# Gated feed-forward input projections: nine of eleven block pairs as seven half-size products, with weight sums on GpSimd

## What is computed

```python
def swiglu(x, w_in, w_out):
    a, b = jnp.split(x @ w_in, 2, axis=-1)
    return (jax.nn.silu(a) * b) @ w_out

for i in range(2):
    h = h + 0.5 * swiglu(rmsnorm(h, g_ff1[i]), w_ff1_in[i], w_ff1_out[i])
    h = h + hybrid_mixer(rmsnorm(h, g_mix[i]), ...)
    h = h + 0.5 * swiglu(rmsnorm(h, g_ff2[i]), w_ff2_in[i], w_ff2_out[i])
    h = h + sigmoid(rmsnorm(h, g_ple[i]) @ w_ple_gate[i]) * (p[i] @ w_ple_proj[i])
```

## Time and profile before

| | |
|---|---|
| median of the runs | 3154.97 us |
| profiled execution, its time | 3155.3 us |
| its span, first to last instruction | 3155.3 us |
| TensorE matmul busy | 3082.0 us (98%) |
| VectorE busy | 1737.8 us (55%) |
| ScalarE busy | 1172.2 us (37%) |
| GpSimd busy | 68.0 us (2%) |
| the chain that ended last | PE 90%, DVE 4%, issue 2%, ACT 2% |

### The profile page before, as it was taken

One profiled execution on the slowest core, in us unless ns is written; L12 is line 12 of the kernel. 1 busy time (PEld: TensorE's weight loads), 2 busy tenths in 40 slices (PEclk: granted clock), 3 DMA queues, 4 the chain that ended last, 5 costly groups with the idle time before them and its releaser, 6 DMA issues.

```text
span 3155.3 us, 42820 instructions
## 1 busy us (share of the span) xinstructions
PE 3082.0 (98%) x17818; PEld 2479.4 (79%) x17818; DVE 1737.8 (55%) x2350; ACT 1172.2 (37%) x1700; POOL 68.0 (2%) x73
## 2 busy tenths in 40 slices
PE   7999999999999999999999999999999999999998
PEld 5777856688888888877888888788888768888886
DVE  5477564534354444687664344743446876643446
ACT  4433243423243223357443223522233474422233
POOL 0012300000000000000000000000000000000000
PEclk9999999999999999999999999999999999999998
DMA  6110045333322322321232323333232212233232
...
DMA packets 83616, 299.29 MB, mean 95 GB/s; under 512 B 9824, under 2 KB 11232, under 8 KB 81504
## 3 DMA queue, kind: packets, MB, share of 16 engines
...
## 4 chain that ended last, share of the span: by engine, by line
PE 90%; DVE 4%; issue 2%; ACT 2%; DMA 0%; SPq 0%; DVEq 0%; ACTq 0%
PE PS L1933 79%; PE PS L2033 3%; PE PS L2283 1%; ACT SPL L2338 1%; PE PS L2267 1%; PE PS L2238 1%; PE PS L1949 1%; DVE SM L2976 1%; PE PS L2226 1%; PE PS L2162 1%; PE PS L2257 0%; PE PS L2292 0%; PE PS L2303 0%; PE PS L2218 0%; DVE CA L3066 0%
## 5 line engine op out<-in xcount | busy, mean ns | idle before, releaser
L1933 PE MATMUL PS<-HS,SPL 128*128 128x512 f32 x7752 | 1799.8, 392 | 7.0 <-DVE HS L2713 3.4
L1933 PEld LDWEIGHTS PS<-HS,SPL 128*128 128x128 f32 x7752 | 1448.9, 188 | 331.1 <-issue 22.0
L2658 DVE TENSOR_TENSOR SPL<-RAW,SPL 128x1024 fp32r<-128x1024 f32 (+1 forms) x483 | 580.3, 1205 | 727.5 <-ACT SPL L2338 723.6
L2338 ACT ACTIVATE SPL<-RAW 128x1024 fp32r<-128x1024 f32 (+1 forms) x483 | 499.3, 1038 | 841.6 <-PE PS L1933 841.2
L1933 PE MATMUL PS<-FF,SPL 128*128 128x512 f32 x2880 | 654.6, 389 | 0.0
L1933 PEld LDWEIGHTS PS<-FF,SPL 128*128 128x128 f32 x2880 | 540.7, 188 | 112.1
L3066 DVE SCALAR_TENSOR_TENSOR CA<-AP__151,CW,CA 128x512 f32<-128x512 f32 x240 | 179.6, 748 | 6.2
L2548 ACT ACTIVATE FF<-TMP 128x512 fp32r<-128x512 f32 x88 | 55.7, 633 | 235.8 <-DVE TMP L3036 235.8
L2542 ACT ACTIVATE SA<-SA 128x512 f32<-128x512 f32 x88 | 55.5, 633 | 191.8 <-DVE SA L3026 191.8
L3026 DVE TENSOR_TENSOR SA<-PS,R 128x512 f32<-128x512 f32 x88 | 60.5, 692 | 98.8 <-PE PS L1933 98.5
L3038 DVE TENSOR_TENSOR FF<-TMP,FF 128x512 fp32r<-128x512 f32 x88 | 60.9, 692 | 66.1 <-ACT FF L2548 66.1
...
## 6 DMA issues: line engine op xcount, KB each, us to landing
RAW<-in_w_ff_in SPq DMA_DIRECT2D x176, 512.0 KB, 3.7
RAW<-in_w_in SPq DMA_DIRECT2D x88, 512.0 KB, 3.7
RAW<-in_w_ff_out SPq DMA_DIRECT2D x80, 512.0 KB, 3.6
RAW<-in_w_ff SPq DMA_DIRECT2D x64, 512.0 KB, 3.7
MW<-in_w_mod SPq DMA_DIRECT2D x32, 512.0 KB, 4.3
RAW<-in_w_out SPq DMA_DIRECT2D x24, 512.0 KB, 3.8
MW<-in_w_mod SPq DMA_DIRECT2D x8, 1024.0 KB, 19.1
RAW<-in_w_ple_gate SPq DMA_DIRECT2D x16, 512.0 KB, 3.9
```

The lines of the kernel that those rows point to most:

```text
L1933: m = pe.matmul(o, w[x][:, r.kp + k, rows], r.T[:, r.k0 + k, y, 0:r.cols], start=r.start and k == 0 and (x, y) == (0, 0), stop=r.stop and ...
L2338: a.activation(SPL[:, s, 0, 0:n], RAW[:, s, 0:n], AF.Copy).then_inc(w_hi, 1)
L2658: v.tensor_tensor(SPL[:, s, 1, 0:n], RAW[:, s, 0:n], SPL[:, s, 0, 0:n], ALU.subtract).then_inc(w_lo, 1)
```

## The change

The input projection of 9 of the 11 block pairs is computed by Strassen's scheme in Winograd's form, over 2x2 blocks: output channels halved (128 each), input channels halved (even and odd tiles), tokens halved (256 each). A block of 256 channels (a or b) is then seven products of 128 channels by 512 input channels by 256 tokens, 12 matmuls of 256 columns each, `product`, instead of 48 matmuls of 512 columns. Pairs 0 and 1 of each call stay dense.

The sums of activations are made once a call (`mixed_tokens`), in four parts, while pairs 0 and 1 run on TensorE: VectorE scales (`halves_in`, now with R and gain), GpSimd makes four sums (`halves_mix`), ScalarE writes high parts (three instructions of `mix_in`), VectorE low parts (three more). The sums of weights are made by GpSimd for each block (`weights_mix`, four instructions of 128x512). The splits of a block are four: A (1024 numbers a partition, raw weights), B and C (1024 each, of the sums) and E (512, raw). Four intermediate PSUM results of 256 tokens are copied out by ScalarE (`keep`), and VectorE adds three (`add_y`, `add_kept`, `add_z`); silu and gate work on quarters. Both RAW slots of a block are refilled when E is split. The chunks of a call are now 4, 4 and 3 pairs.

```diff
+    def raw_piece(src, nk, ncol, even=False):
         p = Rec()
-        p.i, p.src, p.nk, p.ncol, p.lo, p.used, p.next, p.own = len(pieces), src, nk, ncol, None, None, None, []
+        p.i, p.src, p.nk, p.ncol, p.next, p.own, p.mixed = -1, src, nk, ncol, None, [], None
         if not lane or lane[-1] is None:
-            p.slot = 0
+            p.slot = split_turn[0] = 0
         else:
             p.slot = (lane[-1] + 1) % 4
+            if even and p.slot % 2:
+                p.slot = (p.slot + 1) % 4
...
+    def in_ring(p):
+        p.i, p.lo, p.used = len(pieces), None, None
+        p.at = split_turn[0]
+        split_turn[0] = (p.at + 1) % 4
+        p.before = in_split[p.at]
+        in_split[p.at] = p
         pieces.append(p)
         return p
...
+    def mixed_tokens(at, gname, rms):
+        built = []
+        def chunk(c):
+            r = Rec()
+            r.c, r.gname, r.rms, r.H = c, gname, rms, HALF[c % 2]
+            r.parts = lambda y: [(MIX4[at][:, :, c, y, :], r.H[:, 0:4, :]), (MIX2[:, :, c, y, :], r.H[:, 5:7, :]),
+                                 (MIX1[:, c, y, :], r.H[:, 7, :])]
+            r.scaled, r.mixed, r.hi, r.lo = count(s_mu), count(s_zero), count(s_muhi), count(s_mulo)
+            r.over = built[c - 2] if c >= 2 else None
+            built.append(r.lo)
+            def mix():
+                emit("halves_in", r)
+                emit("halves_mix", r)
+                emit("mix_in", r, "ACT")
+            later.append([5 + 2 * c, mix])
+            later.append([8 + 2 * c, lambda: emit("mix_in", r, "DVE")])
+        for c in range(4):
+            chunk(c)
+        return built
+    def fast(src, at, n, history, built, first, evict):
+        F = Rec()
+        F.n, F.keeps = n, [count(s_khi) for _ in range(4)]
+        F.raws = [raw_piece(src[:, a:a + 4, :], 4, 256, a == 0) for a in (0, 4)]
+        s0 = F.raws[0].slot
+        W8 = RAW[:, s0:s0 + 2, :].rearrange("p s (c q m) -> p (s c) q m", c=2, m=256)
+        F.quarter = lambda m, p: W8[:, :, p, m * 128:m * 128 + 128]
+        F.kept = KEPT[at][n % 2]
+        F.T = SUMS[at][n % 2] if n >= 2 else HALF[n].rearrange("p (a b) n -> p a (b n)", a=4)
+        F.sums = [count(s_zero), count(s_zero)]
+        F.back = history[n - 2] if n >= 2 else None
+        F.sums_after = [built[2 + n]] if n < 2 else [first] if n < 4 else []
+        emit("weights_mix", F)
+        F.added = count(s_od)
+        F.X, F.Y, F.Z = single(), single(), single()
+        def unit(sums):
+            p = Rec()
+            p.nk, p.ncol, p.mixed, p.F, p.ends, p.sums = 8, 128, True, F, [], sums
+            in_ring(p)
+            return p
+        A, B, C, E = (unit(x) for x in (None, *F.sums, None))
+        F.units = [A, B, C, E]
+        E.ends = F.raws
+        A.out = lambda x: SPL[:, A.at, x, :].rearrange("p (c q m) -> p c q m", q=2, m=128)
+        A.src = W8[:, :, :, 0:128]
+        for p, t in ((B, 0), (C, 2)):
+            p.out = lambda x, p=p: SPL[:, p.at, x, :]
+            p.src = F.T[:, t:t + 2, :].rearrange("p a n -> p (a n)")
+        E.out = lambda x: SPL[:, E.at, x, 0:512].rearrange("p (c m) -> p c m", m=128)
+        E.src = F.quarter(1, 1)
...
+        def prod(p, half, use, mixed, start, waits):
+            r = Rec()
+            r.p, r.half, r.use, r.T, r.start, r.waits, r.opens = p, half, use, mixed, start, waits, half == 0
+            if start:
+                mark = use.mark
+            else:
+                n_full[use.b] += 1
+                mark = (full[use.b], n_full[use.b])
+            p.used = mark
+            emit("product", r)
+            passed()
+            tick(rate[0])
+            return mark
...
+        m = prod(A, 0, F.X, four(0), True, [built[3]] if n == 0 else [])
+        keep(0, m, F.X, G and G.Y.rel)
+        prod(A, 1, F.Y, four(1), True, [])
+        evict("y", F)
+        emit("add_y", F)
+        give(F.Y)
+        m = prod(B, 0, F.X, four(2), False, [F.keeps[0]])
+        keep(1, m, F.X, G and G.Z.rel)
+        m = prod(B, 1, F.Z, four(3), True, [])
+        keep(2, m, F.Z, G and G.added)
+        if last_lows:
+            emit("quarters_lo", last_lows.pop())
+        m = prod(C, 0, F.X, two(1), False, [F.keeps[1]])
+        keep(3, m, F.X, G and G.added)
+        emit("add_kept", F)
+        F.m_z2 = prod(C, 1, F.Z, two(0), False, [F.keeps[2]])
+        emit("add_z", F)
+        give(F.Z)
+        F.m4 = prod(E, 0, F.X, lambda c, y: MIX1[:, c, y, :], False, [F.keeps[3]])
+        evict("x", F)
+        give(F.X)
+        history.append(F)
+        return F.m4
-        for ci, (a, z) in enumerate([(0, 6), (6, 11)]):
+        at, history = (0 if T is HS2 else 1), []
+        built = mixed_tokens(at, f"{w1[2:5]}_{l}", rms)
+        first = None
+        for ci, (a, z) in enumerate([(0, 4), (4, 8), (8, 11)]):
...
+                if j >= 2:
+                    fast(W[w1][l, j], at, len(history), history, built, first, evict_a)
+                    h_last = fast(W[w1][l, 11 + j], at, len(history), history, built, first, evict_b)
+                    continue
...
+                STEPS.append(("mix_split" if p.mixed else "split", p, None))
...
+        def mix_split(p):
+            for raw in p.ends:
+                if raw.next:
+                    sp.wait_ge(*p.lo)
+                    fetch(raw.next)
...
+            for c in range(4):
+                for x, y in PASSES:
+                    m = pe.matmul(o, SPL[:, p.at, x, p.cols(r.half, c)], r.T(c, y), start=r.start and c == 0 and (x, y) == (0, 0),
+                                  stop=c == 3 and (x, y) == (1, 0), skip_group_check=True)
+            m.then_inc(full[r.use.b], 1)
...
+        def mix_split(p):
+            if p.before:
+                a.wait_ge(*p.before.used)
+            if p.sums:
+                a.wait_ge(*p.sums)
+            else:
+                for raw in p.F.raws:
+                    a.wait_ge(*raw.landed)
+            a.activation(p.out(0), p.src, AF.Copy).then_inc(w_hi, 1)
+        def mix_in(r):
+            a.wait_ge(*r.mixed)
+            for out, src in r.parts(0):
+                m = a.activation(out, src, AF.Copy)
+            m.then_inc(s_muhi, 1)
+        def keep(r):
+            a.wait_ge(*r.mark)
+            if r.after:
+                a.wait_ge(*r.after)
+            a.activation(r.F.kept[:, r.at, :], PS[:, r.b, 0:256], AF.Copy).then_inc(s_khi, 1)
+        def quarters_a(F):
+            s0, s1 = (SA[:, F.sa + i, :] for i in range(2))
+            a.wait_ge(*F.Y.rel)
+            a.wait_ge(*F.Z.rel)
+            a.activation(s0, s0, AF.Silu).then_inc(s_sa, 1)
+            a.wait_ge(*F.m4)
+            a.activation(s1[:, 0:256], PS[:, F.X.b, 0:256], AF.Silu).then_inc(free[F.X.b], 1)
+            a.wait_ge(*F.added)
+            a.activation(s1[:, 256:512], s1[:, 256:512], AF.Silu).then_inc(s_sa, 1)
+        def quarters_b(F):
+            for i in range(2):
+                for w in F.ff_after:
+                    a.wait_ge(*w)
+                a.wait_ge(*F.glu[i])
+                a.activation(FF[:, F.k + i, 0, :], TMP[:, F.slots[i], :], AF.Copy).then_inc(s_ffhi, 1)
...
+        def halves_in(r):
+            v.wait_ge(*r.rms)
+            if r.over:
+                v.wait_ge(*r.over)
+            H4 = r.H[:, :, :].rearrange("p (a b) n -> p b a n", b=4)
+            for i in range(2):
+                m = v.scalar_tensor_tensor(out=H4[:, i, :, :], in0=XT[:, 2 * r.c + i, :].rearrange("p (a n) -> p a n", a=2),
+                                           scalar=vec(r.gname, 2 * r.c + i),
+                                           in1=R[:, :].rearrange("p (a n) -> p a n", a=2), op0=ALU.mult, op1=ALU.mult)
+            m.then_inc(s_mu, 1)
+        def mix_in(r):
+            v.wait_ge(*r.hi)
+            parts_ = list(zip(r.parts(1), r.parts(0)))
+            for (out, src), (hi, _) in parts_:
+                m = v.tensor_tensor(out, src, hi, ALU.subtract)
+            m.then_inc(s_mulo, 1)
+        def add_y(F):
+            dst = F.dst(0)[:, 0:256]
+            for w in F.tmp_after:
+                v.wait_ge(*w)
+            v.wait_ge(*F.Y.mark)
+            v.wait_ge(*F.keeps[0])
+            v.tensor_tensor(dst, PS[:, F.Y.b, 0:256], F.kept[:, 0, :], ALU.add).then_inc(free[F.Y.b], 1)
+        def add_kept(F):
+            v.wait_ge(*F.keeps[3])
+            v.tensor_tensor(F.dst(1)[:, 256:512], F.kept[:, 2, :], F.kept[:, 3, :], ALU.add).then_inc(s_od, 1)
+        def add_z(F):
+            v.wait_ge(*F.m_z2)
+            v.wait_ge(*F.keeps[1])
+            v.tensor_tensor(F.dst(0)[:, 256:512], PS[:, F.Z.b, 0:256], F.kept[:, 1, :], ALU.add).then_inc(free[F.Z.b], 1)
+        def quarters_b(F):
+            t0, t1 = (F.dst(i) for i in range(2))
+            s0, s1 = (SA[:, F.sa + i, :] for i in range(2))
+            v.wait_ge(*F.silu)
+            v.wait_ge(*F.Z.rel)
+            v.wait_ge(*F.Y.rel)
+            v.tensor_tensor(t0, t0, s0, ALU.mult).then_inc(s_glu, 1)
```

(108 more changed lines are left out.)

48 lines of the change are left out of this document (31 added, 17 removed).

## The result

| | before | changed |
|---|---|---|
| median | 3155.5 us | 3346.9 us (3346.3 to 3349.8) |
| ratio | | 1.0604 [1.0589, 1.0619] |
| span of the profiled execution | 3155.3 us | 3345.5 us |
| mean granted clock | 0.993 | 0.964 |

What follows compares the result with a forecast made beforehand. TensorE's matmul stream was taken as the bound (busy 98%). Per call -14.7 us for matmuls, +25.3 for the start and +18.7 for late keeps gave +29.3, +117 over four calls: 3272 us, range 3185 to 3325.

Steps and rivals of the forecast that it cites:

- The price of a product at full clock: TensorE's stream: 256-column matmuls cost 120 ns each against 227 for 512 columns, gaining 14.7 us a call.
- The start of a call: Serial mixing rounds make TensorE wait 1.7 us for piece 7, 18.6 before the first product, 5.0 before B0: 25.3 a call.
- Six late keeps of 3.1 us: After six b blocks a call, B0 of the next block waits 3.1 us on average for keep 0: 18.7 us a call.
- rival 1: VectorE and GpSimd meetings cost nothing, at the start and the late keeps: +14 us a call, 3211 us; chance 0.13.
- rivals 3 and 4: Rival 3: queues keep ahead, 3132 or 3096 us, chance 0.08; rival 4: the start costs half, 3221 us, chance 0.06.
- Rival 3: Mixing rounds of 7.2 us or less, not 10.2 to 13.6, make the start free: 3132 or 3096 us; chance 0.08.
- rival 2: GpSimd dearer: start 33.4 us and late keeps 19.7 a call, 3309 us, half clock up to 18 more; chance 0.12.
- Half clock after such a pause, 0: At a call's start, 24 matmuls at 1.2 GHz hide behind B0's wait: 0, upper bound 4.5 us a call.
- The ends of the range: Whole kernel: 3185 us (rival 1 with a start 6 us a call cheaper) to 3325 (rival 2 with half clock).

Runs made afterwards that it cites:

- e9: Changed kernel with eight pairs by products, three dense, chunks of 3, 4, 4, mixing rounds five passes apart and late evictions: 3136.2 us, ratio 0.9936.
- e2: Changed kernel without the four weight sums of every block, B and C split from raw quarters (values wrong): 3231.0 us, ratio 1.0235.
- e10: e9 with the change's original evictions, SiLU and gating queued before keep 0 of the next block: 3243.4 us, ratio 1.0284.
- e1: Changed kernel with dummy matmuls filling TensorE's pauses before a call's first and third products and after b blocks: 3323.2 us, ratio 1.0527.

## Why the forecast missed, step by step

- **The price of a product at full clock**: right. In full flow 19 lie in 2.00 us and 27 in 3.00 (some at the edges); in e9 the whole group, its last ones before pauses and its cold ones included, is at 122 ns.
- **The start of a call**: right within 1.5 us. 18.3 for 18.6, 1.3 to 1.5 for 1.7, and in the first call B0 2.24 for 5.0 because A0 and A1 took 5.46 us for 2.9: the sum of the two, 7.70, was forecast as 7.9. Here the half clock was indeed hidden, as argued.
- **Six late keeps of 3.1 us**: the place and the cause right, the size a little low (2.8 to 3.9; 20.0 to 22.1 a call in sum, 83 us in all, for 18.7 and 75).
- **No conflict costs anything (rival 1)**: fell; e2 shows 116 us for the sums. **The order is less strict than read (rivals 3 and 4)**: fell for this kernel. Rival 3's condition, rounds that do not hold up the rest, is what e9 brings about.
- **GpSimd dearer (rival 2)**: its condition came in part (weight sums of 1.44 to 1.97 us on average in the four lines, for 1.2), but not its price: the start was no dearer than forecast, and the late keeps cost 20.8 us a call for its 19.7.
- **Half clock after such a pause, 0**: the step that failed. It was weighed for the start of a call alone (24 products, 48 as the bound), where B0 waits anyway, and behind the late keeps not at all. Of the 539 cold products 84 lie in A0 and A1 of the four calls and are hidden, as argued. The other 455, after B0's wait and after the late keeps, are hidden by nothing: 455 x 0.093 us = 42 us, 10.6 a call where 0 stood and 4.5 was the bound. The 25 waits of 2.8 to 3.9 us (24 late keeps and B0 of the fourth call) leave 16 cold products each on average (1 to 26): 1.5 us, nearly half the wait's length again. e10 against e9 shows the pair together, keeps and clock, and e1 the clock alone.
- **The sum of the miss.** Between the spans +190 us was measured where +117 was forecast. Of these 73 us the half clock that nothing hides is 42; the late keeps are 8 longer; small waits are 9; the edges of the pauses 13; some 5 have no place; and the start gives 5 back (88.6 us of waits and 7.8 of hidden half clock, for 101.2).
- Two of these were put at nothing: small waits of 0.4 to 2.6 us a call (0.9 behind a w_out, for the residual's eviction, and 0.2 to 0.4 for a keep) with 0.95 us more behind two of the calls, and the edges of the pauses, which a sum of start-to-start distances doesn't contain. The ends of the range were added loosely too: 3309 + 18 is 3327, and 3211 - 24 is 3187.

Not settled: which of e9's edits at the start (third dense pair, rounds five passes apart, w_out before the first product) carries how much; they were run together. Nor was a start with nine pairs found that has no pause.
